# Moving one more low half per round from VectorE to GpSimd while the experts are chosen

## The reference, cut to what matters

```python
q = (x @ w_q).reshape(n_tok, P_HEADS, 2, P_HALF)
s = jnp.einsum('nhpc,hpkc->nhpk', q, sub_keys)
v1, i1 = lax.top_k(s[:, :, 0], P_TOPK)            # 16 of 128
v2, i2 = lax.top_k(s[:, :, 1], P_TOPK)
cand = (v1[..., :, None] + v2[..., None, :])      # 256 sums
top_s, pos = lax.top_k(cand, P_TOPK)              # the 16 experts of a head
gate = jax.nn.softmax(top_s, axis=-1)
act = gelu(x . u[expert]);  y = sum(gate * act * v[expert])
```

## Time and profile before

| | |
|---|---|
| device time, three runs | 3744.7, 3739.25, 3744.54 us |
| median | 3744.54 us |
| span of the profiled execution (the page gives no time beside it) | 3741.2 us |
| TensorE busy | 3578.3 us, 96% |
| VectorE busy | 2692.4 us, 72% |
| ScalarE busy | 1668.0 us, 45% |
| GpSimd busy | 1017.6 us, 27% |
| TensorE, mean granted clock | 0.983 |
| low halves on VectorE, L2012 | 440, 553.1 us |
| low halves on GpSimd, L1268 | 104, 260.4 us |

### The profile page before, as it was taken

The page is one execution under the profiler, slowest core; times in us unless marked ns, Lnnn a source line. Parts: engine busy times, 40 slices in busy tenths (PEclk is TensorE's granted clock), DMA queues, the critical chain, the costliest instruction groups (busy, mean ns, idle before and its releaser), DMA issues.

```text
span 3741.2 us, 60962 instructions
## 1 busy us (share of the span) xinstructions
PE 3578.3 (96%) x19474; PEld 3054.3 (82%) x19474; DVE 2692.4 (72%) x4731; ACT 1668.0 (45%) x3112; POOL 1017.6 (27%) x740
## 2 busy tenths in 40 slices
PE   8998899999999999998999899899999999999998
PEld 3444599899999999995554496389999999999997
DVE  1543578869996888885886643276967997888886
ACT  2244344457784333334553032135446776333333
POOL 0000243444442222220443000134254443222221
PEclk9999999999999999999999999999999999999999
DMA  6653244598999999992546462235478999999995
GB/s 223 205 175 96 80 128 154 170 339 304 375 381 370 358 346 350 343 348 58 162 154 177 112 166 67 68 101 164 147 268 310 363 375 379 370 348 345 349 344 199
DMA packets 523927, 913.98 MB, mean 244 GB/s; under 512 B 70320, under 2 KB 367408, under 8 KB 515376
## 3 DMA queue, kind: packets, MB, share of 16 engines
q1 hardware_dynamic: 450096, 644.23, 50.5%
q0 software_dynamic: 73728, 268.47, 20.2%
HBM read 782.54 MB, written 130.02 MB: 244 GB/s over the span
## 4 chain that ended last, share of the span: by engine, by line
PE 45%; DVE 5%; DMA 1%; ACT 1%; issue 1%; SPq 0%; POOL 0%; ACTq 0%; DVEq 0%
PE bank L353 9%; PE bank L660 5%; PE bank L661 5%; PE bank L662 5%; PE bank L590 5%; PE bank L592 5%; PE bank L591 5%; PE bank L636 2%; PE bank L786 2%; DVE prod L2292 1%; PE bank L795 1%; DVE X L2294 1%; DVE eq L2049 1%; DVE eq L2056 0%; PE bank L720 0%
## 5 line engine op out<-in xcount | busy, mean ns | idle before, releaser
L590 PE MATMUL bank<-hx,hl 128*128 128x384 f32 (+1 forms) x2304 | 804.6, 349 | 28.2 <-DVE hl L2012 26.5
L591 PE MATMUL bank<-hx,hl 128*128 128x384 f32 (+1 forms) x2304 | 791.2, 343 | 0.0
L592 PE MATMUL bank<-hx,hl 128*128 128x384 f32 (+1 forms) x2304 | 791.2, 343 | 0.0
L660 PE MATMUL bank<-W,hl 128*128 128x384 f32 x2048 | 687.4, 336 | 7.8 <-DVE W L2152 7.8
L662 PE MATMUL bank<-W,hl 128*128 128x384 f32 x2048 | 687.1, 336 | 0.0
L661 PE MATMUL bank<-W,hl 128*128 128x384 f32 x2048 | 687.1, 335 | 0.0
L1291 POOL DMA_INDIRECT rows<-p_v,erow x256 | 262.1, 1024 | 849.6 <-DVE xtok L2159 827.6
L353 PE MATMUL bank<-hT,w_ring 128*128 128x512 f32 x1008 | 452.8, 603 | 30.8 <-DMA w_ring<-b_w_in 19.5
L590 PEld LDWEIGHTS bank<-hx,hl 128*128 128x128 f32 x2304 | 438.3, 190 | 42.9 <-issue 31.8
L1291 POOL DMA_INDIRECT rows<-p_u,erow x256 | 362.4, 1416 | 403.9 <-DVE rows L2085 366.2
L1530 ACT ACTIVATE hl<-hT 128x1024 fp32r<-128x1024 f32 x272 | 287.9, 1059 | 354.9 <-PE bank L662 312.1
(11 more groups left out here) (307 smaller groups left out, 4702.4 us busy)
## 6 DMA issues: line engine op xcount, KB each, us to landing
w_ring<-p_u_t SPq DMA_DIRECT2D x128, 512.0 KB, 6.0
hT<-p_u_t SPq DMA_DIRECT2D x128, 512.0 KB, 6.0
w_ring<-p_v SPq DMA_DIRECT2D x128, 512.0 KB, 6.6
hT<-p_v SPq DMA_DIRECT2D x128, 512.0 KB, 6.9
act_scratch<-hT SPq DMA_DIRECT2D x256, 192.0 KB, 4.4
g_scratch<-gst SPq DMA_DIRECT2D x48, 1024.0 KB, 6.9
gg<-g_scratch SPq DMA_DIRECT2D x64, 768.0 KB, 7.4
ua<-act_scratch SPq DMA_DIRECT2D x256, 192.0 KB, 5.6
```

The lines of the kernel that those rows point to most:

```text
L590: nc.tensor.matmul(bank[s][:, c:], hi, hx[:, 0, k, c:], start=(k == 0), stop=False)
L591: nc.tensor.matmul(bank[s][:, c:], hi, hx[:, 1, k, c:], start=False, stop=False)
L592: mm = nc.tensor.matmul(bank[s][:, c:], lo, hx[:, 0, k, c:], start=False, stop=(k == KD - 1))
L660: nc.tensor.matmul(bank[j][:, P:], hi, W[:, s, 0, :], start=first, stop=False)
```

## The change

In the 8 helped rounds GpSimd makes the low halves of slots 0, 1 and 2 (`three_lows`), VectorE that of slot 3 only. The two calls for slot 1 in `choices` are gone; the two for slot 3 stay where they were. `t.turn("split3")` counts the slot that is left to VectorE.

```diff
-                def even_lows(n):
+                def three_lows(n):
                     with t.loop(n, {"split0": 1, "split1": 1, "split2": 1, "split3": 1}):
-                        for s in (0, 2):
+                        for s in range(3):
                             low(s)
-                            t.turn(f"split{s + 1}")
+                        t.turn("split3")
...
                 four_lows(UNHELPED)
-                even_lows(HELPED)
+                three_lows(HELPED)
                 pool.wait_ge(sem("rows_stage"), 3 * l + 1)
...
                 def choices(i):
-                    low_ahead(1, i * 2 + UNHELPED)
                     step(nc.vector.tensor_copy(cS[:, :, :], cand[:, ds(i * PH, PH), :]))
...
                     step(ins)
-                    low_ahead(1, i * 2 + (UNHELPED + 1))
                     for h in range(0, PH, 2):
```

## The result

The kernel after the change took 3767.55 us (median), beside 3744.62 us for the kernel before on the same chip: a ratio of 1.0055, with a 95% interval of 1.0037 to 1.0074, or +20.6 us; the two medians themselves lie 22.9 us apart. The ratio leaves out one disturbed execution of 11846.55 us, without which the median is 3767.39 us. The profiled execution took 3776.43 us, with a span of 3774.7.

A forecast was written before the change was run, and what follows sets the result against it. VectorE was taken to set the pace while experts are chosen, TensorE elsewhere. 11.1 + 0.8 + 15.8 - 2 + 2.3 = 28.0 us, put on the median 3744.54, gives 3772.5 us; 8-in-10 range 3744 to 3785.

The forecast's parts named there:

- the count of meetings in a pass: In `choices`, five of six GpSimd low halves a pass hold up a VectorE instruction (a meeting), 2.15 us each.
- The anchor: A, VectorE's first slot-3 low half of a pass: ready at 579.74, within 0.28 us, before and after alike.
- Price 2.15 us each: VectorE's loss when a GpSimd low half meets its two-input instruction: 2.15 us, mean of 2.20, 2.20 and 2.05.
- Pass 42.4 us: One pass of `choices` on VectorE, two rounds: 33.95 - 2.3 + 5 x 2.15 = 42.4 us.
- One wait of TensorE a pass, for B, some 8 us: In the stage TensorE waits for every B, VectorE's second slot-3 low half of a pass, some 8 us each.
- 20 meetings and a stretch of 153.7 us: Per layer, first to eighth slot-3 low half: 118.7 - 8.0 + 43.0 = 153.7 us, 20 meetings costing the 43.0.
- The clock and layer 1's slack, +1.1 together: Slow TensorE clock after the last wait adds 0.8 us in layer 0, 2.3 in layer 1; layer 1 slack takes 2 off.
- GpSimd has room: Three low halves take GpSimd 7.2 to 11.2 us of a 16.6 us round; cost nothing.
- loads cost nothing: SyncE's load into slot 1 can start earlier, into slot 3 later; TensorE waits for no such load: nothing.
- The faster rival: GpSimd's extra low halves fall in safe stretches of VectorE: 16 us less over both layers, 3728.5; chance 0.15.
- No change at one meeting in two: Half the extra GpSimd low halves meet, costing 8.0 us, just what VectorE saves: 3744.5; chance 0.13.
- Still slower by the clock: TensorE becomes the bound at its lower clock in `choices`: 16 to 20 us more, 3791; chance 0.10.

The follow-up runs named there:

- e1: The changed kernel with GpSimd's slot-1 low half left out in the helped rounds, only its semaphore raised: 3731.0 us, ratio 0.9952 to the kernel before.
- e7: The kernel before plus one GpSimd subtraction a helped round, two buffers into a third, 2.40 us like a low half: 3768.6 us, ratio 1.0065.
- e9: The changed kernel with all three GpSimd low halves of the helped rounds left out, waits and semaphores kept: 3707.0 us, ratio 0.9885 to the kernel before.
- e6: The changed kernel with the second slot-3 call of a pass two instructions earlier, mid L2054: 3731.2 us, ratio 0.9959 to the kernel before.
- e4: The kernel before with all four low halves of the helped rounds on GpSimd, none in `choices`: 3717.8 us, ratio 0.9928.
- e3: The kernel before plus one GpSimd memset of 0.96 us per helped round, in an unused buffer: 3751.3 us, ratio 1.0017.
- e2: The kernel before plus one in-place GpSimd subtraction of 1.90 us per helped round, in an unused buffer: 3759.2 us, ratio 1.0039.

## Why the prediction was right

- **The step that carried it, the count of meetings in a pass, was right.** Five in six were predicted, and the rows at 586.40 to 620.34 show five in six, in the order given: slots 0, 1, 2, 0 and 1 meet, slot 2 behind B is safe. Only the first of them fell later than predicted, never on A: 3.6 us behind A in the first pass and at 627.05 in the second, 16.5 us after B had let TensorE go and not 15. It met L2048 instead, at the same price. e1, e7 and e9 show that the meetings are the cause, not only company. The anchor held too: A moved from 579.74 to 582.78, 3.0 us, which is how much later the whole stage began.
- **Price 2.15 us each:** measured 2.01 to 2.23 in `eq` and 1.94 to 2.14 in the low half, 2.15 on average over the 36 meetings of the two stretches. By the rule of the Trainium skill, SBUF — State Buffer, section Who interferes with whom, the engine that starts first blocks the other for its whole instruction. The turns shown above agree with it, but for the size: the whole 2.40 would be lost, and this trace gave some 0.2 to 0.5 us less. GpSimd's own instruction grew as well, from 2.40 to as much as 4.08, by its wait for the running one.
- **Pass 42.4 us:** measured 42.7, 42.7 and 42.5. **One wait of TensorE a pass, for B, some 8 us:** one a pass, but shorter, 5.4 to 7.5 and at the last B 3.1 (2.9 in layer 1). TensorE stopped at the tile of slot 3, as assumed.
- **20 meetings and a stretch of 153.7 us:** too many. Both layers took 150.2, with 18 meetings. The first three passes had five each, the last one three: from 726.14 on GpSimd issued its gathers, not low halves, while VectorE was in L2054, which ran 9.02 us (one meeting), and the low half of 732.98 was free. The text had put the gathers behind the eight rounds, but not into the last pass. That is 2 x 2 x 2.15, or 8.6 us on paper and 7.0 by the stretches (2 x 3.5).
- **The clock and layer 1's slack, +1.1 together:** nothing measurable. M grew by 7.4 and 12.5, the stretches by 7.6 and 12.4. So 28.0 - 7.0 - 1.1 = 19.9, which is the growth of M: the term that was mis-sized is the number of meetings in the last pass.
- **"GpSimd has room", "loads cost nothing":** right; in this stage TensorE waited for no low half of GpSimd's and for no load.
- **The faster rival**, safe places for slot 1, is real (e6), but not here. **No change at one meeting in two:** excluded, 15 of 18 in three passes met. **Still slower by the clock:** the clock fell to 0.88 to 0.92 in these passes, but a pass stayed at 42.7, since VectorE, not TensorE, set it.
- **Two figures of the text were loose.** VectorE's 39.2 us a pass is the mean of four windows (38.83 to 39.43). And 16 to 22 meetings at 2.05 to 2.40 us give 3752 to 3792 us at the corners, not the 3755 to 3784 of the forecast's own range. Neither touches the result.
- What the prediction didn't see is that VectorE needn't be in this chain at all. It priced a meeting wherever it fell, as right in its own kernel; e4 shows that the price lapses once no low half stands behind.

## What to carry to other kernels

Work moved from VectorE to GpSimd wasn't free for VectorE here, since both read SBUF: count how many of the moved instructions will run beside two-input instructions or copies of VectorE, and pay nearly the whole GpSimd duration for each that delays something another engine waits for. Moving a part of such work can lose where moving all of it wins, because the last piece takes the slow queue off the critical path. Before pricing contention, ask who waits for the engine that is held up, and how evenly the things waited for are spaced in its queue.

## What the runs showed of the hardware

- A memset on GpSimd inside a held-up `eq` cost VectorE nothing (e3), a subtraction in the same place 1.7 to 2.2 us (e2, e7).
- A copy of VectorE is held up as well: 2.40 us for 0.22 (e6), and five of the 20 meetings before the change fell on copies.
- The meetings fall by phase, and a small shift changes their number: the same kernel had 11 and 9 in its two layers before, and 18 and 18 after; one call moved by two instructions (e6) took the stretch from 150.2 to 134.7 us, of which 3.5 are the two instructions that no longer lie in it, and M down by 15.4 in that layer. An experiment that adds a disturbance (e2) therefore understates it.
- Both engines lose, by taking turns. In all kernels with meetings GpSimd's low half ended 2.20 to 2.29 us after the VectorE instruction inside which it had started (once, in e1, after the following one, which began 0.01 us behind it), and a held-up instruction of `eq` 1.68 or 1.69 us after GpSimd's. With four low halves meeting one `eq` (e4, 15.65 us for 7.03), three of GpSimd's took 3.65 to 3.93 us and still kept pace with TensorE's tile of 4.16 us (a quarter of 16.64).
